# A decoder layer on one core: a seventh set of expert weights, one gather buffer, and eight value pages loaded outside the ring

## The reference

```python
h = rmsnorm(x); z = h @ w_in                      # 1024 x 9216: rq rk rv rg | aq ak av | gates
A: retention, 4 heads (128 x 256 state), chunks of 128, rotary, group norm, silu(rg) gate
B: MoBA attention, 8 heads of 128: top 3 of the past blocks of 256 keys by q . mean(k), plus the own block
merged = sigmoid(gr) * (A @ w_ret_o) + sigmoid(ga) * (B @ w_att_o);   x = x + merged @ w_o
h2 = rmsnorm(x)
group = argmax(h2 @ w_rg + b_rg) of 4; two best of its 8 experts; weights = group prob * softmax
x = x + sum_e combine_e * (silu(h2 @ w_gate[e]) * (h2 @ w_up[e])) @ w_down[e]   # 32 experts, hidden 256
y = rmsnorm(x)
```

## Time and profile before

| | |
|---|---|
| median of 3 runs | 768.91 us (768.21 to 770.3) |
| profiled execution | 769.54 us, span 767.7 us |
| TensorE busy | 653.7 us (85%) |
| VectorE, ACT, POOL busy | 308.1, 141.3, 139.2 us |
| DMA | 243.00 MB, mean 317 GB/s |
| chain that ended last | PE 55%, DMA 26%, DVE 14% |

### The profile page before, as it was taken

One profiled execution on the slowest core, in us unless ns is written; L12 is line 12 of the kernel. 1 busy time (PEld: TensorE's weight loads), 2 busy tenths in 40 slices (PEclk: granted clock), 3 DMA queues, 4 the chain that ended last, 5 costly groups with the idle time before them and its releaser, 6 DMA issues.

```text
span 767.7 us, 13776 instructions
## 1 busy us (share of the span) xinstructions
PE 653.7 (85%) x5037; PEld 459.7 (60%) x5037; DVE 308.1 (40%) x1554; ACT 141.3 (18%) x404; POOL 139.2 (18%) x209
## 2 busy tenths in 40 slices
PE   6999999999899987989998999827996848767593
PEld 4888887787788765744433877626654525443341
DVE  3005988998867775610000221444324201111114
ACT  3222223223235222210010000121110101000012
POOL 0169954761000223200000000011000000000000
PEclk9999999999999999999999999958998969787898
DMA  9939899789978999579999989457699999999971
GB/s 306 273 110 321 284 305 393 263 280 354 360 252 269 338 322 350 171 276 402 399 410 383 291 330 381 174 225 266 245 392 401 388 387 401 402 403 399 415 283 58
DMA packets 93830, 243.00 MB, mean 317 GB/s; under 512 B 8786, under 2 KB 54482, under 8 KB 85442
## 3 DMA queue, kind: packets, MB, share of 16 engines
q1 hardware_dynamic: 56818, 192.99, 67.1%
q10 hardware_dynamic: 31328, 32.00, 12.8%
q0 software_dynamic: 5616, 17.11, 6.5%
HBM read 235.00 MB, written 9.11 MB: 318 GB/s over the span
## 4 chain that ended last, share of the span: by engine, by line
PE 55%; DMA 26%; DVE 14%; issue 2%; SPq 1%; ACT 1%; POOL 0%; DVEq 0%; ACTq 0%; POOLq 0%
PE zps L885 31%; DVE kall L1367 7%; DMA qb<-in_w_down 6%; DMA hT<-in_w_down 6%; PE zps L1202 4%; PE nps L1179 4%; PE nps L1054 4%; DMA ring_all<-in_w_ret_o 4%; DMA ring_all<-in_w_down 3%; DMA out<-sfin 2%; PE nps L856 2%; DMA kall<-in_cache_k 2%; DMA gain<-v_rows 2%; PE zps L856 1%; PE bps L1217 1%
## 5 line engine op out<-in xcount | busy, mean ns | idle before, releaser
L885 PE MATMUL zps<-hT,ring_all 128*128 128x264 f32 x1152 | 276.3, 394 | 1.6 <-DVE hT L1548 1.0
L885 PEld LDWEIGHTS zps<-hT,ring_all 128*128 128x128 f32 x1152 | 218.3, 194 | 45.6 <-issue 5.6
L1367 DVE CUSTOM_DVE_ANT_0 kall<-kall,qb 128x128 f32<-128x128 f32 x512 | 153.2, 366 | 59.8 <-DMA kall<-in_cache_k 57.1
L596 POOL DMA_INDIRECT zatt<-h_rows,tidx_i x16 | 15.1, 943 | 361.3 <-DVEq L1636 199.8
L1054 PE MATMUL nps<-ring_all,zret 128*64 128x512 f32 x256 | 59.1, 600 | 5.4 <-DMA ring_all<-in_cache_v 4.3
L885 PE MATMUL zps<-headT,ring_all 128*128 128x264 f32 x256 | 58.5, 388 | 4.9 <-DMA ring_all<-in_w_ret_o 3.5
L885 PEld LDWEIGHTS zps<-headT,ring_all 128*128 128x128 f32 x256 | 48.2, 190 | 16.0 <-issue 6.0
L1709 DVE TENSOR_TENSOR qdT<-qdT,nps 128x64 f32<-128x64 f32 x32 | 7.1, 221 | 118.6 <-ACT qdT L801 118.1
L645 ACT ACTIVATE zt<-zps 128x264 f32<-128x264 f32 x56 | 21.8, 390 | 153.6 <-PE zps L885 147.5
L1535 DVE TENSOR_TENSOR hT<-zps,zatt 128x264 f32<-128x264 f32 x8 | 3.5, 433 | 96.4 <-PE zps L885 96.3
L1367 DVE DVE_READ_ACCUMULATOR2_ANT scores<- 128x1 f32 x512 | 40.9, 80 | 0.0
(11 more groups left out here) (360 smaller groups left out, 829.1 us busy)
## 6 DMA issues: line engine op xcount, KB each, us to landing
kall<-in_cache_k SPq DMA_DIRECT2D x64, 512.0 KB, 6.5
ring_all<-in_cache_v SPq DMA_DIRECT2D x64, 512.0 KB, 8.1
ring_all<-in_w_in ACTq DMA_DIRECT2D x26, 1024.0 KB, 8.4
ring_all<-in_w_gate SPq DMA_DIRECT2D x12, 1024.0 KB, 18.8
ring_all<-in_w_up SPq DMA_DIRECT2D x12, 1024.0 KB, 21.8
ring_all<-in_w_down SPq DMA_DIRECT2D x12, 1024.0 KB, 14.5
ring_all<-in_w_in SPq DMA_DIRECT2D x6, 1024.0 KB, 13.5
kall<-in_w_gate SPq DMA_DIRECT2D x5, 1024.0 KB, 22.6
```

The source lines that it names most:

```text
L596: pool.indirect_dma_start(out=rows, out_offset=None, in_=h2_rows, in_offset=bass.IndirectOffsetOnAxis(ap=col, axis=0), bounds_check=T - 1, ...
L885: mm = pe.matmul(zps[m % 2][:, 0:T], w[:, k, P * fb:P * (fb + 1)], rhs[:, k, :], start=(k == 0), stop=(k == KT - 1))
L1367: ins = v.tensor_tensor_reduce(kh, kh, qb[b % 2][:, P * h:P * (h + 1)], 1.0, 0.0, ALU.mult, ALU.add, scores[:, pg, AH * b + h:AH * b + h + 1])
```

## The change

The text of the change, cut to its core:

```diff
-ADD_AT = {(q, half): 4 * q + 5 + half + 2 * (q == 0) for q in range(NQUAD - 1) for half in range(2)}
+ADD_AT = {(q, half): 4 * q + 6 + half + 2 * (q == 0) for q in range(NQUAD - 1) for half in range(2)}
-SETS = 6
+SETS = 7
+V_SOON = 4
...
-        order += [("v", k) for k in range(N_V) if min(k // 8, 2) == j]
+        order += [("v", k) for k in range(V_SOON, N_V) if min(k // 8, 2) == j]
...
+        rows_a, rows_b = sb("rows_a", [P, DM]), sb("rows_b", [P, DM])
...
+        v_soon = [kall[:, 0:2048], kall[:, 2048:4096], zdec_all[:, 0:2048], zdec_all[:, 2048:4096]]
-        xg = [zflat[0:2 * CAP, DM * i:DM * (i + 1)] for i in range(2)]
-        ysb = zflat[:, 2 * DM:3 * DM]
+        xg = rows_b[0:2 * CAP, :]
+        ysb = rows_a
-        gate_up_w.append(headT[:, :, 0:2048])
+        gate_up_w += [headT[:, :, 0:2048], zflat[:, 0:4096].rearrange("p (a c) -> p a c", a=2)]
-                  scr[:, 0:2048], qb_all[:, :, :].rearrange("p a b -> p (a b)")]
+                  scr[:, 0:2048], qb_all[:, :, :].rearrange("p a b -> p (a b)"), cst[:, COL["causal"][0]:COL["causal"][0] + 2048]]
-        xgT = [zflat[:, 3 * DM + 512 * i:3 * DM + 512 * (i + 1)] for i in range(2)]
+        xgT = [gain[:, 512 * i:512 * (i + 1)] for i in range(2)]
...
                     for p in range(NB * NPG):
                         key_page(p)
+                        if p == 53:
+                            sp.wait_ge(f_nT, 1)
+                            sp.wait_ge(out_done, 96)
+                            sp.wait_ge(d_T, 1)
+                            sp.wait_ge(v_out, 16)
+                            for j in (2, 3):
+                                value_pages(j, v_soon[j], v_soon_in[j])
+                    for j in range(2):
+                        sp.wait_ge(page_done, NB * NPG - 2 + 2 * j)
+                        value_pages(j, v_soon[j], v_soon_in[j])
...
             down_in(1, 1)
+            down_in(6, 6)
...
             down_in(5, 5)
-            for e in range(SETS, NE + 2):
-                if e < NE:
-                    sp.wait_ge(e_GU, e + 1 - SETS)
-                    gate_up_in(e % SETS, e)
-                if e >= SETS + 2:
-                    sp.wait_ge(e_D, 2 * ((e - 2 - SETS) // 4 + 1))
-                    down_in((e - 2) % SETS, e - 2)
+            sp.wait_ge(h2_out, 48)
+            gate_up_in(6, 6)
+            def next_down(e):
+                sp.wait_ge(e_D, 2 * ((e - SETS) // 4 + 1))
+                down_in(e % SETS, e)
+            downs = SETS
+            for e in range(SETS, NE):
+                sp.wait_ge(e_GU, e + 1 - SETS)
+                gate_up_in(e % SETS, e)
+                while downs <= min(e - (4 if e < 16 else 2), NE - 5):
+                    next_down(downs)
+                    downs += 1
+            for e in range(downs, NE - 4):
+                next_down(e)
+            sp.wait_ge(e_D, 2 * ((NE - 1 - SETS) // 4 + 1))
+            for half, signals in enumerate((d_in, None)):
+                for e in range(NE - 4, NE):
+                    sp.dma_start(down_w[e % SETS].rearrange("p (f n) -> p f n", f=FB)[:, :, 512 * half:512 * (half + 1)],
+                                 w_down[0, bass.ds(e, 1), :, 512 * half:512 * (half + 1)].rearrange("o (f p) n -> p (o f) n", p=P)
+                                 ).then_inc(signals[e % SETS] if signals else d_last, 16)
...
+            sp.wait_ge(e_GU, NE)
+            sp.dma_start(gain[:, :], norm_final.rearrange("(o d) -> o d", o=1).partition_broadcast(P)
+                         .rearrange("p o d -> p (o d)")).then_inc(fgain, 16)
...
-            for p in range(2):
-                gather_for(p)
-            for p in range(2, NPAIR):
-                gather_for(p)
+            for p in range(NPAIR):
+                if p:
+                    pool.wait_ge(e_T, p)
+                gather(xg, tidx_i[0:2 * CAP, p:p + 1])
...
-                if e >= 4 and e % 4 < 2:
-                    quad_down(e // 4 - 1, e % 4)
+                if e >= 5 and e % 4 in (1, 2):
+                    quad_down(e // 4 - 1, e % 4 - 1)
-                if e == 6:
+                if e == 7:
                     residual_in()
...
-            link(v.memset(st[:, 14:15], 1.0))
-            link(v.tensor_tensor_reduce(fbuf[1][0:NB, :], xs[0:NB, 2, :], xs[0:NB, 2, :], 1.0, 0.0, ALU.mult, ALU.add, st[0:NB, 14:15]))
+            act.activation(fsq, xs[0:NB, 2, :], ACT.Square, accum_out=st[0:NB, 14:15]).then_inc(f_sq, 1)
```

More of the change, by code:

```diff
@@ L511, in turn @@
                 link(pool.tensor_tensor(x2, x2, tb, ALU.add))
+            for lo, hi in ((0, T), (328, 584), (648, DM)):
+                link(pool.memset(rows_b[0:2 * CAP, lo:hi], 0.0))
             a0, _ = COL["rope"]
@@ L617, in _ @@
                     pool.wait_ge(pchain, j + (base + 1))
-                    pool.sem_inc(pool_turn, 1)
-                    gather(0, xg[0][0:CAP, :], tcol[0:CAP, 0:1])
+                    pool.sem_inc(past_wait, 1)
+                    gather(xg[0:CAP, :], tcol[0:CAP, 0:1])
             pool.wait_ge(out_done, 16 * 6)
@@ L1047, in values @@
             def values(j):
-                n = AT["v", j]
                 b = j // 4
-                pe.wait_ge(slot_in[n % RING], slot_value(n))
+                if j < V_SOON:
+                    pages = v_soon[j]
+                    pe.wait_ge(v_soon_in[j], 32)
+                else:
+                    n = AT["v", j]
+                    pages = ring[n % RING]
+                    pe.wait_ge(slot_in[n % RING], slot_value(n))
                 for k in range(2):
```

129 lines of the change are left out of this document (64 added, 65 removed).

## The result

The changed kernel takes 763.4 us in the median of 20 runs (757.62 to 769.25) and the kernel before 768.93 in 20 runs (765.89 to 773.62). The ratio is 0.9912, with a 95% interval of 0.9894 to 0.9929; it is not the quotient of the two medians, which lie 5.5 us apart, and it leaves out the slowest of the 20 runs (769.25), which counts as slow. So the change makes the kernel faster by 6.8 us, give or take 1.4, where 17.8 were forecast. The sign was right, the size was not: a good third came, and the median lies just above the range, which ended at 763. The profiled execution took 763.91 us, with a span of 762.1.

What follows compares the result with a forecast made beforehand. Transfers were taken to set the pace in the value pages and experts; +1 - 3 - 7 - 9 + 1.7 - 1.5 = -17.8 us from the profiled 769.54 gave 751.7, so 751 for the median, range 739 to 763.

Steps and rivals of the forecast that it cites:

- A: Value pages 4 to 7 behind key page 53: some transfers spill onto small ones on the path, +1 us (0 to +4).
- B: Fewer transfers in 282 to 298, so TensorE's stalls at the state updates halve: -3 us (0 to -6.2).
- C: Value stage: early value units shorten it despite two idle gaps, -7 us (-8 to -3).
- The first gap: Value stage: DMA engines idle some 4 us, as unit 9 can be issued only when unit 4 is used.
- the prediction's own sign of being wrong: Wrong if the value stage shortens under 4 us, DMA share falls over 3 us between e_D 2 and 14, or gathers exceed 10.
- D: Start of the experts: seven fewer transfers left at e_D 2, -19.6, which comes later, +11: taken as -9 us (-16 to -2).
- E: Tail: gate-up 31 lands later and the four last downs are issued only after e_D 14, +1.7 us.
- rival 2: Experts give the gain back: DMA engines idle at the first three down waits or the last; D near 0, 760 us; 17%.
- The final chain: End of the kernel: ACT takes the sample square from VectorE, 1.21 us, and some links: -1.5 us.
- Rival 4: Experts: the single gather buffer becomes the bound and the kernel slower, 782 us at 12 us a gather; 6%.

Runs made afterwards that it cites:

- e2: The changed kernel without the early value pages, all 32 value units in the ring as before; ratio 0.9917 to the kernel before.
- e7: e3 with the four value pages that stood behind key page 53 issued behind value unit 4; ratio 0.9833 to the kernel before.
- e3: The changed kernel with the four value units outside the ring used last, not first; ratio 0.9879 to the kernel before.
- e4: The changed kernel with two gather buffers again, in two halves of the partitions of `rows_b`; ratio 0.9863 to the kernel before.
- e5: The changed kernel with downs 28 to 30 loaded whole behind e_D 12, only the last in halves behind e_D 14; ratio 0.9877 to the kernel before.
- e6: The changed kernel with gate-up 6 issued when the first gather has landed, not when the rows are written; ratio 0.9913 to the kernel before.
- e8: The changed kernel with the edits of e7, e4, e5 and e6 together; 750.3 us, ratio 0.9735 to the kernel before.
- e12: e8 without the edit of e6, so gate-up 6 again goes out beside the first gather; 754.9 us, ratio 0.9777 to the kernel before.
- e9: The changed kernel with the first down's halves back behind gate-ups 5 and 6; ratio 0.9885 to the kernel before.
- e13: e8 with gate-up 31 issued ahead of down 28; ratio 0.9748 to the kernel before.

## Why the prediction missed

Of the 12.2 us between forecast (span 749.9) and profile (762.1), by the prediction's own steps:

- **A and B: forecast -2, measured +0.9** in the pair of profiles, and -0.2 to -1.0 with the means over kernels (V 333.8 in the seven with early pages, 334.0 in the two profiles of the kernel before, 334.8 with e2); so 1 to 2 us of the pair are scatter. B came as foreseen (-2.9 for -3). A was mis-sized: +1 was taken between 0 and +4, and it is 2 to 3 (the wait is 4.6 us in the mean with early pages, 2.0 with the old order; V moves by 2.3). The prediction named the path itself, the small transfers from `sfin` and into `gain`, and then let 2.5 of the 5.2 us of pages "fit in" by the mean share of a window. A share of 0.79 says how full the engines are, not when the small transfers come; they met the pages, as e7 shows.
- **C: forecast -7, measured -2.8.** The first gap was foreseen in place and nearly in size; e3 shows what using the units last gives back, about 2. The step that failed is the line behind it, "unit 13 then lands at 359.6, and 18 value units and the last two of `w_ret_o` follow at 2.62". Unit 13 landed at 362.8, 27.8 us after V where 25.5 were counted: from the end of `w_ret_o` 1's pair (356.2) to its landing it took 6.5 us and not 4.1, with its pages issued one after the other. The 20 transfers behind it took 2.72 us each and not 2.62, with shares of 0.9 up to 365. So behind the gap the ring was taken as refilled at the full rate; it refilled at shares of 0.75 and 0.92, since SP issues a page only when TensorE has used a unit. This makes 2.3 and 1.9 us of the miss. It is also where the prediction's own sign of being wrong came true, a stage C shorter by less than 4 us; the other two, an idle stretch of over 3 us between e_D 2 and e_D 14 and gathers of over 10 us, did not. The best that any kernel here reached in this stage is -5.2 (e3).
- **D: forecast -9, measured -6.7** (what E leaves of the 2.3 us between 236.9 and 234.6). e_D 2 came 12.2 us later than in the first profile of before, 10.4 later than in the second; forecast 11. From e_D 2 to e_D 14 it took 170.9 us, where 57 transfers at 2.80 and 10.5 us make 170.1. This step was nearly right. The idle time at e_D 6 was rival 2's and real, 1.3 us in 611 to 617, but not shown to cost anything, since e2 and e3 have no such hole and the same 171 us. e4 shows that the one gather buffer makes TensorE wait in later pairs too, which the prediction had left to the first three.
- **E: forecast +1.7, measured +4.4**: from e_D 14 to the end 18.0 us, where the prediction had 15.3 (+25.8 less +10.5). The term that failed is the landing of the four last downs, "1.5 us to start and four transfers": the second halves land 15.9 us after e_D 14 where 12.1 were counted. The start itself was priced about right, as the share is 0.98 from 730 on, though the eight halves are issued one by one over 4 us (728.32 to 732.36). The transfers behind it then took 14.3 us and not 10.6. At a share of 1.00 they moved 363 GB/s in 730 to 742 and not 400, part of the half megabyte of `gain`, issued at 733.75, among them, and then the share falls to 0.48 and 0.12 before the last half is there; no run separates these. e5 shows that 3.9 us go when only one of the four downs waits.
- **The final chain: forecast -1.5, measured -1.4** (from the last down's end to the span's: 15.8 against 17.2).

The misses are 2.9 + 4.2 + 2.3 + 2.7 + 0.1 = 12.2, of which 1 to 2 are scatter of this pair. No term had the wrong mechanism; four had the wrong size, all to the same side. C and E counted what a transfer costs or saves when the engines are full, and let the stretches in which they fill up and run dry cost too little. Rival 2, at 760, was the nearest number, partly by luck. It named idle engines at the first three down waits or at the last. They do idle at the last (0.51 in 725 to 731) and, without a shown cost, at e_D 6; but D gave 6.7 us where this rival had it near 0, and the value stage, which it left at -7, gave less. Rival 4 didn't come: no gather of the changed kernel took over 8.5 us, and none in any run over 9.2.

## What to carry to other kernels

A head start in a stage that transfers set is worth its bytes only if the buffers that it leaves behind are refilled at once: use the early ones last, or the ring behind them stands full and idle. Price the first transfers behind a wait by how they are issued, one after the other, and not by the full rate, and count the end to the landing of the last one, when the share has long begun to fall; and let only that load wait for an event whose buffer needs it. And an edit that is worth nothing alone can be worth 3 to 4 us beside another one, when alone it only moves a collision onto what the other takes away (e6 alone; e8 against e12).

## What the runs showed of the hardware

- The same small gather lands 3.5 to 4.2 us after its issue with idle DMA engines, and 7.40 with only gate-up 6's two transfers beside it (the first one of the changed kernel), 7.6 and 7.0 for the first two in e12, 8.6 for the second one of e6: it does not take a full queue. The Trainium skill (DMA: Bandwidth & Descriptors, Queues, rings and completion order) has the engines take turns between queues packet by packet; that fits a gather which slows down by a factor of about two and hardly further: the longest in all runs took 9.2 us (e4).
- TensorE's gate-up of 64 small matmuls takes 1.95 us at the granted clock of 1.00 (2.4 GHz) and 3.64 at 0.50 (1.2 GHz, e9 at 519.17). In the changed kernel the clock stands at 0.50 in 500 to 520, after the router, where TensorE is busy for 4.73 us of the first 12 and 0.80 of the last 8, and comes back in the first pairs, at another gate-up in each profile. That may be why e_D 2 scatters by a microsecond or two between profiles of the same order; no run here tells it.
- Profiles of the same order repeat a stage that full transfers set to about 1 us (the value stage 81.5 to 82.3 in six kernels, 80.4 to 81.6 in e7, e8, e12 and e13), and the way to V, with retention's small transfers in it, only to 4.5 us (330.8 to 335.3).
